# An encoder trunk on one Trainium2 core: squares after the rounded tiles, products of ones at the outset, and a third result buffer

## The reference

```python
u = rmsnorm(h, norm_g[l])                      # h / sqrt(mean(h*h) + eps) * gain
p = u @ w_in[l]                                # 1024 -> 9216
hq, hf_f, hf_b, hi, hgt, aq, ak, av, agt = split(p)
o_h = hgrn2_mixer(hq, hf_f, hf_b, hi, hgt, ...)            # 8 heads, linear recurrence, both directions
o_a = diff_attention_mixer(aq, ak, av, agt, ...)           # 8 heads, two softmaxes and their difference
h = h + concat(o_h, o_a) @ w_out[l]            # 2048 -> 1024
```

## Time and profile before

| | |
|---|---|
| median of 3 runs | 1490.86 us (1490.78 to 1490.89) |
| the profiled execution | 1490.87 us |
| its span | 1488.9 us |
| TensorE busy | 1471.6 us, 99% |
| VectorE busy | 1064.6 us, 72% |
| ScalarE busy | 810.9 us, 54% |
| granted clock, mean | 0.999 |

### The profile page before, as it was taken

One profiled execution on the slowest core, in us unless ns is written; L12 is line 12 of the kernel. 1 busy time (PEld: TensorE's weight loads), 2 busy tenths in 40 slices (PEclk: granted clock), 3 DMA queues, 4 the chain that ended last, 5 costly groups with the idle time before them and its releaser, 6 DMA issues.

```text
span 1488.9 us, 28116 instructions
## 1 busy us (share of the span) xinstructions
PE 1471.6 (99%) x11216; PEld 1401.9 (94%) x11216; DVE 1064.6 (72%) x1819; ACT 810.9 (54%) x1736; POOL 90.6 (6%) x109
## 2 busy tenths in 40 slices
PE   7999999999999999999999999999999999999998
PEld 7999999999999999999999999999999889999987
DVE  7777777777664777777577777778776657777754
ACT  6555545655433565566554555565654445665654
POOL 0000000000000000000100000000001000000010
PEclk9999999999999999999999999999999999999999
DMA  6112111111222222222232121221212232222222
GB/s 208 59 57 67 63 58 57 58 57 58 77 67 88 84 72 72 72 67 66 70 101 86 57 71 58 63 67 57 71 58 72 72 105 81 72 72 82 76 84 73
DMA packets 34561, 109.94 MB, mean 74 GB/s; under 512 B 4864, under 2 KB 4992, under 8 KB 34432
## 3 DMA queue, kind: packets, MB, share of 16 engines
q1 hardware_dynamic: 34432, 108.15, 23.4%
HBM read 97.38 MB, written 2.10 MB: 67 GB/s over the span
## 4 chain that ended last, share of the span: by engine, by line
PE 95%; DVE 2%; ACT 1%; issue 1%; DMA 0%; SPq 0%; DVEq 0%; ACTq 0%
PE proj L1558 65%; PE pair L1676 8%; PE meta L1786 4%; PE pair L1771 2%; PE pair L1773 2%; PE main L1800 2%; PE meta L1788 1%; PE main L1741 1%; PE main L1742 1%; PE pair L1722 1%; PE main L1654 1%; PE main L1683 1%; PE pair L1729 1%; PE main L1745 1%; PE pair L1708 0%
## 5 line engine op out<-in xcount | busy, mean ns | idle before, releaser
L1558 PE MATMUL proj<-u_hi,w_hi 128*128 128x264 f32 (+1 forms) x2048 | 495.0, 313 | 9.5 <-DVE w_lo L1080 8.0
L1558 PE MATMUL proj<-u_lo,w_hi 128*128 128x264 f32 (+1 forms) x2048 | 465.3, 298 | 0.0
L1558 PE MATMUL proj<-u_hi,w_lo 128*128 128x264 f32 (+1 forms) x2048 | 465.3, 298 | 0.0
L1558 PEld LDWEIGHTS proj<-u_hi,w_hi 128*128 128x128 f32 x2048 | 326.7, 190 | 22.2 <-DVE w_lo L1080 8.0
L1558 PEld LDWEIGHTS proj<-u_hi,w_lo 128*128 128x128 f32 x2048 | 326.0, 189 | 11.2
L1558 PEld LDWEIGHTS proj<-u_lo,w_hi 128*128 128x128 f32 x2048 | 326.4, 189 | 7.7
L1080 DVE TENSOR_TENSOR w_lo<-w_raw,w_hi 128x1024 fp32r<-128x1024 f32 x178 | 218.9, 1230 | 49.9 <-ACT w_hi L682 49.8
L682 ACT ACTIVATE w_hi<-w_raw 128x1024 fp32r<-128x1024 f32 x178 | 186.7, 1050 | 64.1 <-PE proj L1558 62.6
L902 ACT ACTIVATE decay<-pair,neg_max 128x528 f32<-128x528 f32 (+1 forms) x144 | 100.4, 697 | 218.5 <-DVE neg_max L1425 218.3
L1425 DVE TENSOR_REDUCE neg_max<-pair 128x1 f32<-128x528 f32 (+1 forms) x144 | 101.4, 704 | 110.7 <-PE pair L1773 110.5
L834 ACT ACTIVATE q_level<-ops 128x528 f32<-128x528 f32 (+1 forms) x112 | 76.5, 683 | 86.0 <-DVE ops L1327 85.8
(11 more groups left out here) (216 smaller groups left out, 2206.5 us busy)
## 6 DMA issues: line engine op xcount, KB each, us to landing
w_raw<-w_units SPq DMA_DIRECT2D x178, 512.0 KB, 3.5
q_stack<-gate_f SPq DMA_DIRECT2D x32, 132.0 KB, 2.3
k_stack<-k_stack SPq DMA_DIRECT2D x32, 132.0 KB, 2.3
h<-x_t SPq DMA_DIRECT2D x8, 264.0 KB, 5.4
cos_sin<-rope SPq DMA_DIRECT2D x2, 528.0 KB, 6.5
out_t<-ops SPq DMA_DIRECT2D x2, 512.0 KB, 3.5
out_t<-decay SPq DMA_DIRECT2D x2, 512.0 KB, 4.0
masks<-level_masks SPq DMA_DIRECT2D x1, 448.0 KB, 6.0
```

Source lines behind the costliest of these rows:

```text
L1558: ins = pe.matmul(out, w, x[:, tile, cols_n], start=(k == 0 and p == 0), stop=(k == last_k and p == 2))
```

## The change

Three things, most of them at the outset of layer 0.

- ScalarE rounds all eight tiles and the weights of units 0 and 1, and only then squares the tiles; VectorE makes all `u_lo`, `cut_low` of units 0 and 1 and the exponents' preparation, and then adds the squares. The weights of unit 2 are cut last.
- TensorE begins with 18 products of `ones` with itself (fp32, 128 x 128, into `main`), which nobody reads.
- The sums of squares move into unit 1: after its piece 6 in layer 0 (KT - 2), after its piece 1 in layer 1. They go to `far`, which is `main` and `meta` as one tensor. Unit 2 of each layer goes to `pair` in place of `proj`, and waits for no evacuation; in layer 1 it waits for the last reader of `pair` in layer 0 (`last_added`).

```diff
+THIRD_UNIT = 2
+WARM_UP = 18
...
-        main = ctx.enter_context(nc.psum_tensor("main", [P, 512], f32))
-        meta = ctx.enter_context(nc.psum_tensor("meta", [P, 512], f32))
+        far = ctx.enter_context(nc.psum_tensor("far", [P, 2, 512], f32))
+        main, meta = far[:, 0, :], far[:, 1, :]
...
+        def result(t):
+
+            return pair if t % LAYER_UNITS == THIRD_UNIT else proj[t % 2]
...
-                act.activation(two(rms_inv[:, :]), pair[:, :, both], ACT.Sqrt, bias=eps_count[:, :])\
+                act.activation(two(rms_inv[:, :]), far[:, :, both], ACT.Sqrt, bias=eps_count[:, :])\
...
                 cut_u_high(0, k)
                 if k == 0:
                     cut_high(0)
+            cut_high(1)
+            for k in range(KT):
                 square_h(0, k)
-            for u in range(1, N_CUT):
+            for u in range(2, N_CUT):
                 cut_high(u)
             root(0)
...
                 cut_u_low(0, k)
                 if k == 0:
                     cut_low(0)
-                if 1 <= k < KT - 1:
-                    add_squares(0, k)
+            cut_low(1)
             prepare_exponents()
-            for u in range(1, N_CUT):
+            for k in range(1, KT - 1):
+                add_squares(0, k)
+            for u in range(2, N_CUT):
                 cut_low(u)
...
                     pe.wait_ge(lo_cut, t + 1)
-                    if t >= 2:
+                    if i == THIRD_UNIT:
+                        if l > 0:
+                            pe.wait_ge(last_added, l * (EARLY_TILES - 1))
+                    elif t >= 2:
                         pe.wait_ge(evacuated[t % 2], evac_count(t - 2))
...
+            def warm_up():
+
+                pe.wait_ge(ones_set, 1)
+                for _ in range(WARM_UP):
+                    pe.matmul(main[:, 0:P], ones[:, :], ones[:, :], start=True, stop=True)
...
-                for k in range(KT):
-                    piece(l, 0, k)
-                    if k == (KT - 1 if l == 0 else KT // 2):
-                        sum_squares(l)
-                for i in range(1, len(HG_TILES)):
+                if l == 0:
+                    warm_up()
+                for i in range(len(HG_TILES)):
                     for k in range(KT):
                         piece(l, i, k)
+                        if i == 1 and k == (KT - 2 if l == 0 else 1):
+                            sum_squares(l)
```

More of the change, by code:

```diff
@@ L526, in normed @@
             return slice(N_META if n == DEPTH else 0, T)
-        def normed_halves(n):
-            return ((0, slice(0, SEQ), normed(n)),) if n == DEPTH else \
-                tuple((b, both, keys) for b, keys in enumerate(halves))
         def rows_out(j):
@@ L1144, in evacuate @@
                     dst = v_t[:, :]
-                dve.tensor_tensor(rows_of(l, what, dst), grown(l, what, proj[t % 2]), rows_of(l, what, rms_inv),
+                dve.tensor_tensor(rows_of(l, what, dst), grown(l, what, result(t)), rows_of(l, what, rms_inv),
                                   ALU.mult).then_inc(evacuated[t % 2], 1)
@@ L1556, in piece @@
                     for n, cols_n in enumerate((slice(N_META, T),) if short(l, what) else halves):
-                        out = proj[t % 2][:, n, 0:SEQ if short(l, what) else HALF]
+                        out = result(t)[:, n, 0:SEQ if short(l, what) else HALF]
                         ins = pe.matmul(out, w, x[:, tile, cols_n],
@@ L1584, in sum_squares @@
             def sum_squares(n):
-                if n == 0:
-                    pe.wait_ge(ones_set, 4)
                 pe.wait_ge(h_sq_added, (n + 1) * (KT - 2))
-                for b, cols_out, cols_n in normed_halves(n):
-                    pe.matmul(pair[:, b, cols_out], ones[:, :], sq[:, cols_n], start=True, stop=False)
+                for b, keys in enumerate(halves):
+                    pe.matmul(far[:, b, both], ones[:, :], sq[:, keys], start=True, stop=False)
                 pe.wait_ge(h_sq, (n + 1) * KT)
-                for b, cols_out, cols_n in normed_halves(n):
-                    ins = pe.matmul(pair[:, b, cols_out], ones[:, :], decay[:, (KT - 1) % 4, cols_n],
+                for b, keys in enumerate(halves):
+                    ins = pe.matmul(far[:, b, both], ones[:, :], decay[:, (KT - 1) % 4, keys],
                                     start=False, stop=True)
                 ins.then_inc(h_sq_summed, 1)
+            def warm_up():
+                pe.wait_ge(ones_set, 1)
+                for _ in range(WARM_UP):
+                    pe.matmul(main[:, 0:P], ones[:, :], ones[:, :], start=True, stop=True)
             def half_piece(b, k):
```

## The result

| | before | changed |
|---|---|---|
| median of 20 runs | 1490.82 us (1490.28 to 1492.32) | 1493.20 us (1491.23 to 1495.53) |
| the profiled execution | 1490.87 us | 1494.54 us |
| its span | 1488.9 us | 1492.6 us |
| granted clock, mean | 0.999 | 0.998 |

The ratio is 1.0015, with a 95% interval of 1.0009 to 1.0021: the change costs 2.4 us. My forecast was 1491.1, in a range to 1492.0. So the sign of the shift was right and its size was not (for a shift of 0.2 us the sign is little to be proud of), and the executions lie much further apart than those of the kernel before.

What follows compares the result with a forecast made beforehand. TensorE was taken to bound the kernel, never lacking work outside its start-up. The profiled 1490.87 us plus 0.66 lost in layer 0 minus 0.44 gained in layer 1 gave 1491.09, say 1491.1, range 1490.0 to 1492.0.

Steps and rivals of the forecast that it cites:

- Part 1: Outset of layer 0: no tile late for unit 0; unit 1 waits 0.9 us for its weights, begins at 14.77, before 19.19.
- Part 2: Start of TensorE: 18 products of ones end near 7.0, or 8.98 if slow; they buy at most 0.9 at unit 1.
- (c): Rival, chance 0.15: clock falls back or never rose before 8.0; unit 0 ends at 15.69, total 1491.6 us.
- (d): Rival, chance 0.05: slow products of ones hold TensorE to 8.98, sums at 23.6, total 1492.6 us.
- Part 3: Layer 0, unit 1: adds end at 20.19, sums at 22.12; root, reciprocal and VectorE's following work come 2.93 us later.
- Part 4: Layer 0, unit 3: waits for unit 1's evacuation; TensorE idles 2.76 us, unit 3 at 31.57 against 30.91, 0.66 us lost.
- Part 5: Layer 1's outset: sums moved after piece 1 of unit 1, a 0.5 wait on u_lo replaces 0.8; 0.44 us gained.
- (a): Rival, chance 0.06: unit 3 finds proj[1] free, TensorE keeps 2.2 + 0.44, total 1488.2 us.
- Theory F: From the experiments: 72 added instructions cause a late instruction fetch that holds the last store, costing half a microsecond.

Runs made afterwards that it cites:

- e3: The changed kernel without its 18 products of ones: 1493.64 us, +2.9 against the kernel before.
- e9: e5 without the 18 products of ones: 1489.51 us, -1.4 against the kernel before.
- e1: The changed kernel with prepare_lower_bounds moved behind unit 1's evacuation on VectorE: 1489.70 us, -1.1 against the kernel before.
- e5: As e1, with the weights of unit 3 also cut before the root and the reciprocal: 1489.23 us, -1.6 against the kernel before.
- e7: The kernel before with only layer 1 changed (sums after piece 1 of unit 1, unit 2 in pair): 1490.38 us, -0.5 against the kernel before.
- e0: The changed kernel measured again, unaltered: 1493.38 us, +2.6 against the kernel before.
- e17: The changed kernel with 5 products of ones of 512 columns in place of its 18: 1493.21 us, +2.3 against the kernel before.
- e11: e5 measured again on another occasion: 1489.38 us, -1.5 against the kernel before.
- e12: e5 with 5 products of ones of 512 columns in place of 18 of 128: 1488.67 us, -2.1 against the kernel before.
- e14: e9 measured again on another chip: 1488.79 us, -2.0 against the kernel before.
- e10: The changed kernel with 5 products of ones put between units 2 and 3 of layer 0: 1491.82 us, +0.9 against the kernel before.
- e6: The changed kernel with unit 2 of layer 0 in proj[0], waiting for unit 0's evacuation: 1496.33 us, +5.5 against the kernel before.
- e8: The kernel before with only the 18 products of ones added: 1491.20 us, +0.3 against the kernel before.
- e16: e8 measured again on another chip: 1491.15 us, +0.2 against the kernel before.

## Why the prediction was wrong, point by point

- **Part 1, u tiles first**: right. Unit 0 is never late for a tile, unit 1 waits for its weights' DMA and begins at 14.72 for 14.77.
- **Part 2, the ones**: right in their own time (they end at 6.9, 7.0 was put down) and in the fast pieces behind them. Neither (c) nor (d) came to be in the profiled execution. What I called the most they can buy, 0.9 at unit 1, reaches the end as no more than e3 and e9 show: 0.1 to 0.3 in the medians, within the noise.
- **Part 3, adds and sums**: the mechanism right, a term mis-sized. The six adds run from 15.75 to 20.51: the last five take 3.96, a pitch of 0.81, where I had 0.74. The gap behind an add that waits for its own engine's semaphore is 0.1, and the 0.04 that I took was that of a wait across two engines. It makes the sums 0.33 late, one to one on all that follows.
- **Part 4, the new wait**: place, cause and length right (2.7 for 2.76; unit 3 at 31.89, where the sum counts from 31.57), and e1 and e5 confirm the cause by removing it. **Here the sum failed**: I priced idle time of TensorE at its length. The unit behind it took 7.39 for 5.86, 1.53 more, as the granted clock fell to 0.50. The price stood in my own rows: the first pieces of the kernel before, 1.34 each in place of 0.733 after an engine that had done nothing. In (c) I asked whether the clock would fall back in the 1.0 us between the ones and the first piece, and not the same of a wait almost three times as long that I was adding myself. The earlier trace rows could have warned: the kernel before has no wait above 0.8 us behind its first product, so no row showed what a longer one does. With 0.33 and 1.53 added to the 1491.09, the sum is 1492.95, for an execution in which the clock falls.
- **Part 5, layer 1**: right as far as the trace tells: 0.44 forecast, 0.49 by e7's median (within its noise), 0.60 by its last transpose; the wait on u_lo is 0.36 for 0.5.
- **The rivals**: (a) did not happen for the reason given. The rival that won was not among them: one that keeps the forecast's wait and adds the clock.
- **What is left**: the fall comes in part of the executions, so the time has two groups. By the sum they should lie near 1491.4 (1491.09 and 0.33) and 1492.95; the medians of the times of the two groups are 1492.1 and 1493.7. So both lie 0.7 above the sum. Part of it lies outside the traced span: the median spans are 1489.8 and 1491.5, 0.35 and 0.5 above the sum, and the nine executions of the first group take 2.5 us more than their spans, where the kernel before takes 1.9. The marks of e0 do not show it (last transpose 1.81 later than before, where the sum has 0.99 + 1.53 - 0.44 = 2.08), and its place within the span was not found. Theory F explains it in part at most: e17, with 20 added instructions, has times no more than 2.0 above their spans, and its median is that of the changed kernel all the same, with 8 of its 11 spans in the long group.

## What to carry to other kernels

A wait that a change puts on the engine which bounds the kernel costs its length, and if it is TensorE and the wait is longer than any that the trace has behind its start, the slow clock behind it as well: take the pitch of the kernel's first products as its price. That is read from waits of 2.7 and 4.4 us and from none between 1.6 and 2.7. Starting a chain earlier on one engine is worth only what the next engine's queue can follow; here 2.2 us of TensorE were lost behind 2.4 us of tiny steps on VectorE that used to be hidden, moving them behind the evacuation turned a loss of 2.4 us into a gain of about 1 (e1), and cutting one unit's weights ahead of the reciprocal as well made it 1.4 to 2.1 (e5, e9, e11, e12, e14). If such a wait can't be removed, filling it with products that nobody reads kept the clock up (1.5 us).

## What the runs showed of the hardware

- Idle times of TensorE of 0.3 to 0.9 us (all kernels), of 1.4 us behind the ones (e5) and of 1.6 us (e10) left the fast pitch of 0.24 to 0.25 a pair behind them; 2.7 us brought the clock to 0.50 in the profiled executions of the changed kernel, e0, e3 and e17 and, judged by the two groups of spans, in 39 of the 53 executions of these four; 4.4 us (e6) in the profiled one, and all six have mean clocks of 0.996 to 0.998. The Trainium skill ("TensorE: Matmul & The Clock Gate", part "Why this matters for your kernels") advises against idle gaps above about 3 us between bursts of products; the runs are a little stricter, as 2.7 us were too long already. The same page (part "What's actually happening") says that the number of slow products at the start varies from run to run. The traces agree: the 18 products of ones took 7.20 us in e8 and 5.90 in e16, which are the same kernel.
- fp32 products of one column are no cheaper than those of 128: 7.84 us for 18, 0.44 each. And after them the first three pieces ran slow (0.44 a pair, from 8.68), where after 5.7 to 7.4 us of products of 128 or 512 columns they ran fast.
- An operation of VectorE that waits for the semaphore of the one just before it followed at 0.81 us, being 0.70 long (the adds of squares in the changed kernel).
